# Three-layer kernel on one NeuronCore: layer norms by token tile, with the two matmul units ahead of them interleaved

## The reference

```
u = x @ w_in[l]                     # conv, two attentions, gates
m = g0 * conv(u) + g1 * diff_attention(u) + g2 * moba_attention(u)
x = layer_norm(ALPHA * x + m @ w_o[l])
h = square(relu(x @ w_ff1[l] + b_ff1[l]))
x = layer_norm(ALPHA * x + h @ w_ff2[l] + b_ff2[l])
```

## Time and profile before

| | |
|---|---|
| median of three runs | 1439.31 us |
| the profiled execution | 1438.97 us |
| its span, first to last instruction | 1437.2 us |
| TensorE busy | 1326.4 us (92%) |
| VectorE busy | 882.1 us (61%) |
| ScalarE busy | 599.6 us (42%) |
| mean granted TensorE clock | 0.963 |

### The profile page before, as it was taken

One profiled execution on the slowest core, in us unless ns is written; L12 is line 12 of the kernel. 1 busy time (PEld: TensorE's weight loads), 2 busy tenths in 40 slices (PEclk: granted clock), 3 DMA queues, 4 the chain that ended last, 5 costly groups with the idle time before them and its releaser, 6 DMA issues.

```text
span 1437.2 us, 22986 instructions
## 1 busy us (share of the span) xinstructions
PE 1326.4 (92%) x9406; PEld 1152.1 (80%) x9406; DVE 882.1 (61%) x1410; ACT 599.6 (42%) x957; POOL 33.1 (2%) x51
## 2 busy tenths in 40 slices
PE   7999989799999899998989999879889859999995
PEld 6999889698898799987979998778778746666563
DVE  3999867765555699985875545656874652222223
ACT  4346663444444434666435444435354322212211
POOL 1000000000000000000000000020040000000000
PEclk9999999999999999999999999979899969999998
DMA  9754435375555364443546555464346629999980
GB/s 291 251 177 145 142 88 160 132 231 189 175 185 194 124 226 150 148 134 100 172 147 199 197 179 199 143 193 147 105 145 225 226 117 377 415 419 419 415 355 31
DMA packets 172582, 289.96 MB, mean 202 GB/s; under 512 B 10324, under 2 KB 143076, under 8 KB 160204
## 3 DMA queue, kind: packets, MB, share of 16 engines
q1 hardware_dynamic: 169580, 281.55, 56.2%
q0 software_dynamic: 2752, 7.07, 1.7%
q10 hardware_dynamic: 160, 0.08, 0.0%
HBM read 287.61 MB, written 3.16 MB: 202 GB/s over the span
## 4 chain that ended last, share of the span: by engine, by line
PE 64%; DVE 26%; ACT 5%; issue 3%; DMA 1%; DVEq 0%; SPq 0%; ACTq 0%; POOL 0%
PE ps L1568 15%; PE ps L1569 14%; PE ps L1570 14%; DVE w_lo L995 8%; PE ps L1961 8%; DVE cvh L1113 5%; PE ps L1983 4%; ACT w_hi L630 3%; PE ps L1945 2%; PE ps L1992 2%; DVE nm L1071 1%; DVE x_nat L1044 1%; DVE gT L1036 1%; DVE ro L1105 1%; DVE ro L1101 1%
## 5 line engine op out<-in xcount | busy, mean ns | idle before, releaser
L995 DVE TENSOR_TENSOR w_lo<-raw,w_hi 128x2048 fp32r<-128x2048 f32 (+1 forms) x170 | 378.5, 2226 | 176.1 <-ACT w_hi L630 175.9
L630 ACT ACTIVATE w_hi<-raw 128x2048 fp32r<-128x2048 f32 (+1 forms) x170 | 316.8, 1864 | 265.7 <-PE ps L1570 259.4
L1568 PE MATMUL ps<-xT_hi,w_lo 128*128 128x256 f32 (+1 forms) x1224 | 356.7, 291 | 9.3 <-DVE xT_lo L1013 7.1
L1569 PE MATMUL ps<-xT_lo,w_hi 128*128 128x256 f32 (+1 forms) x1224 | 349.6, 286 | 0.0
L1570 PE MATMUL ps<-xT_hi,w_hi 128*128 128x256 f32 (+1 forms) x1224 | 349.2, 285 | 0.0
L1568 PEld LDWEIGHTS ps<-xT_hi,w_lo 128*128 128x128 f32 (+1 forms) x1224 | 237.1, 194 | 20.7 <-issue 11.7
L1569 PEld LDWEIGHTS ps<-xT_lo,w_hi 128*128 128x128 f32 (+1 forms) x1224 | 237.4, 194 | 0.5
L1570 PEld LDWEIGHTS ps<-xT_hi,w_hi 128*128 128x128 f32 (+1 forms) x1224 | 237.0, 194 | 0.2
L1568 PE MATMUL ps<-w_hi,xT_lo 128*128 128x256 f32 (+2 forms) x560 | 171.2, 306 | 2.0 <-DVE w_lo L995 1.7
L1569 PE MATMUL ps<-w_lo,xT_hi 128*128 128x256 f32 (+2 forms) x560 | 168.4, 301 | 0.0
L1570 PE MATMUL ps<-w_hi,xT_hi 128*128 128x256 f32 (+2 forms) x560 | 168.4, 301 | 0.0
(11 more groups left out here) (367 smaller groups left out, 1893.3 us busy)
## 6 DMA issues: line engine op xcount, KB each, us to landing
raw<-in_w_in SPq DMA_DIRECT2D x72, 1024.0 KB, 5.1
raw<-in_w_ff SPq DMA_DIRECT2D x64, 1024.0 KB, 5.2
raw<-in_w_gate SPq DMA_DIRECT2D x10, 1024.0 KB, 7.4
raw<-in_w_up SPq DMA_DIRECT2D x10, 1024.0 KB, 8.9
w_exp<-in_w_down SPq DMA_DIRECT2D x10, 1024.0 KB, 9.9
raw<-in_w_o SPq DMA_DIRECT2D x8, 1024.0 KB, 4.9
w_exp<-in_w_gate SPq DMA_DIRECT2D x8, 1024.0 KB, 9.1
raw<-in_w_down SPq DMA_DIRECT2D x8, 1024.0 KB, 10.3
```

What stands on the lines that cost most here:

```text
L630: nc.scalar.activation(w_hi[:, u % SPLIT, 0:n], raw[:, u % RAW, 0:n], ACT.Copy).then_inc(hi_done, 1)
L995: nc.vector.tensor_tensor(w_lo[:, u % SPLIT, 0:n], raw[:, u % RAW, 0:n], w_hi[:, u % SPLIT, 0:n].bitcast(F32), ALU.subtract).then_inc(spli ...
L1568: nc.tensor.matmul(out_, left[1], right[0], start=start, stop=False)
L1569: nc.tensor.matmul(out_, left[0], right[1], start=False, stop=False)
```

## The change

- **Last two units by tile** (`last_rows`). Of the two units ahead of a layer norm, TensorE now does: tile 0 of the first, tile 0 of the second, tile 1 of the first, tile 1 of the second. The second unit's operands are waited for after tile 0 of the first.
- **A third slot** (`w_ext`). The second of these units is split into a part of `br_hi` and `br_lo` that is free then, and the units after it change slots, so that the next stage's first unit can be split ahead of the norm.
- **The norm by tile.** Mean, squares, inverse root (`rsqrt_row`, 8 tiny steps for one tile) and outputs of tile 0 come ahead of the additions of tile 1.
- **Transposes by tile and half** (`turn`): one PSUM bank holds the four transposed blocks of one tile and half. In the third layer the order is half first.
- **High parts first.** The first column block of the first unit after a norm does its 16 matmuls with `xT_hi` first, and then the 8 with `xT_lo`. It waits for three of four parts of `xT_hi` (two in the third layer).
- The load of the third layer's first gain is released one output earlier.

```diff
+        BY_TILE = [(a, h) for a in range(TT) for h in range(2)]
+        BY_HALF = [(a, h) for h in range(2) for a in range(TT)]
+
+        def turned(a, h):
+
+            return ps[:, ACC + 2 * a + h, :].rearrange("p (c t) -> p c t", c=4)
+
+        def xT_part(x, a, h):
+
+            return x[:, 4 * h:4 * h + 4, a * P:(a + 1) * P]
+
+        w_ext = [x[:, 1:3].rearrange("p b c t -> p (b c t)") for x in (br_hi, br_lo)]
+
+        def split_of(u):
+
+            if u in (U_WO + 3, UNITS - 1):
+                return w_ext
+            slot = (u + (U_WO + 3 < u < UNITS - 1)) % SPLIT
+            return w_hi[:, slot, :], w_lo[:, slot, :]
+
+        def slot_user(u):
+
+            if u in (U_WO + 3, UNITS - 1):
+                return U_WO - 1
+            return u - 3 if u in (U_FF, U_FF + 1, UNITS, UNITS + 1) else u - 2
...
             def hi(base, u, n=UCOLS, i=None):
 
-                turn = (base + u) if i is None else (base + i + u)
-                act.wait_ge(unit_done, turn + 1)
-                nc.scalar.activation(w_hi[:, u % SPLIT, 0:n], raw[:, u % RAW, 0:n], ACT.Copy).then_inc(hi_done, 1)
+                turn = base + slot_user(u)
+                act.wait_ge(unit_done, (turn if i is None else turn + i) + 1 + SPLIT_CREDIT)
+                nc.scalar.activation(split_of(u)[0][:, 0:n], raw[:, u % RAW, 0:n], ACT.Copy).then_inc(hi_done, 1)
...
-                squares(0)
+                squares(0, 0)
                 split_hi(U_FF + 1)
+                squares(0, 1)
...
+                for q in range(2):
+                    u = UNITS - 5 + 2 * q
+                    relu(u, FFJ - 2 + q, 0, q)
+                    split_hi(u + 2)
+                    square_hi(FFJ - 2 + q, q)
+                    split_hi(u + 3)
+                squares(1, 0)
                 split_hi(UNITS + 1)
+                squares(1, 1)
...
+            def rsqrt_row(total, n, eps, v, y, z):
+
+                link(nc.vector.tensor_scalar(v, total, -(2.0 ** 26) / n, -(2.0 ** 26) * eps, ALU.mult, ALU.add))
+                link(nc.vector.tensor_scalar(y.bitcast(I32), v.bitcast(I32), -0.5, float(0x1F3759DF), ALU.mult, ALU.add))
+                for c in (3.0, 12.0, 768.0):
+                    link(nc.vector.scalar_tensor_tensor(out=z, in0=y, scalar=y, in1=v, op0=ALU.mult, op1=ALU.mult))
+                    link(nc.vector.scalar_tensor_tensor(out=y, in0=z, scalar=c, in1=y, op0=ALU.add, op1=ALU.mult))
...
-                    dve.wait_ge(ln_var, l * 2 * TT + k * TT + TT)
-                    link(last)
-                    link(nc.vector.tensor_scalar(nw[:, 0, 0:TT], ln_sq[:], 1.0 / D, LN_EPS, ALU.mult, ALU.add))
-                    rsqrt(nw[:, 0, 0:TT], nw[:, 1, 0:TT], nw[:, 2, 0:TT])
-                    for h in range(2):
-                        cols = slice(h * BANK, (h + 1) * BANK)
-                        for a in range(TT):
+                        dve.wait_ge(ln_var, l * 2 * TT + k * TT + a + 1)
+                        link(last)
+                        rsqrt_row(ln_sq[:, a:a + 1], D, LN_EPS, *[nw[:, i, a:a + 1] for i in range(3)])
+                        for h in range(2):
+                            cols = slice(h * BANK, (h + 1) * BANK)
                             nc.vector.scalar_tensor_tensor(out=x_nat[:, a, cols], in0=ln_y[:, a, cols], scalar=nw[:, 1, a:a + 1], in1=lnb[:, 1, cols], op0=ALU.mult, op1=ALU.add).then_inc(x_out, 1)
...
+                for k in range(3):
                     split(base, U_WO + k + 2, UCOLS)
                 layer_norm(0, U_WO + 3)
-                split(base, U_FF)
...
+                for q in range(2):
+                    u = UNITS - 5 + 2 * q
+                    square(FFJ - 2 + q, q)
+                    split(base, u + 2)
+                    square_lo(FFJ - 2 + q, q)
+                    split(base, u + 3)
                 layer_norm(1, UNITS - 1)
-                split(base, UNITS)
...
+                if ready is not None:
+                    o = ps[:, bank, 0:T]
+                    for k in range(KC):
+                        if k % 4 == 0:
+                            pe.wait_ge(xT_hid, ready[k // 4])
+                        nc.tensor.matmul(o, w[1][:, k, 0:P], xT[0][:, k, :], start=k == 0, stop=False)
+                        nc.tensor.matmul(o, w[0][:, k, 0:P], xT[0][:, k, :], start=False, stop=False)
+                    for k in range(KC):
+                        if k % 4 == 0:
+                            pe.wait_ge(xT_lod, ready[k // 4])
+                        nc.tensor.matmul(o, w[0][:, k, 0:P], xT[1][:, k, :], start=False, stop=k == KC - 1)
...
+            def last_rows(u, left, second_ready, second_left):
+
                 for a in range(TT):
                     for h in range(2):
-                        for k in range(2):
-                            last = mm3(ps[:, ACC + 2 * a + h, :], [x[:, k, a * P:(a + 1) * P] for x in left],
-                                       [x[:, k, h * BANK:(h + 1) * BANK] for x in w], start and k == 0, stop and k == 1)
-                        if stop and (a, h) != (TT - 1, 1):
-                            last.then_inc(tile_done, 1)
-                last.then_inc(unit_done, 1)
+                        last = rows_part(u, a, h, left, False, False)
+                    if a == 0:
+                        second_ready()
+                    else:
+                        last.then_inc(unit_done, 1)
+                    for h in range(2):
+                        last = rows_part(u + 1, a, h, second_left, False, True)
+                        last.then_inc(unit_done if (a, h) == (TT - 1, 1) else tile_done, 1)
...
+                def turn(a, h):
+                    for c in range(4):
+                        last = nc.tensor.transpose(turned(a, h)[:, c, :], x_nat[:, a, (4 * h + c) * P:(4 * h + c + 1) * P], ident[:])
+                    last.then_inc(xT_done, 1)
...
                 def make_xT(k):
-                    for half in range(2):
-                        pe.wait_ge(x_out, l * 8 + 4 * k + 2 * half + 1)
-                        for c in range(4 * half, 4 * half + 4):
-                            for a in range(TT):
-                                last = nc.tensor.transpose(ps[:, ACC + c // 2, (c % 2) * T + a * P:(c % 2) * T + (a + 1) * P], x_nat[:, a, c * P:(c + 1) * P], ident[:])
-                            if c % 2 == 1:
-                                last.then_inc(xT_done, 1)
+                    for b, (a, h) in enumerate(BY_TILE):
+                        pe.wait_ge(x_out, X_CREDIT + l * 8 + 4 * (k - 1) + b + 1)
+                        turn(a, h)
...
+                for a, h in BY_HALF:
+                    cols = slice(h * BANK, (h + 1) * BANK)
+                    nc.vector.scalar_tensor_tensor(out=dst[:, a, cols], in0=x_nat[:, a, cols], scalar=nw[:, 1, a:a + 1], in1=gain[:, cols], op0=ALU.mult, op1=ALU.mult).then_inc(normed, 1)
...
+                m_of = [[x[:, 2 * k:2 * k + 2, :] for x in xT] for k in range(4)]
+                for k in range(2):
+                    mixed_ready(k)
+                    rows_unit(U_WO + k, m_of[k], k == 0, False)
+                mixed_ready(2)
+                last_rows(U_WO + 2, m_of[2], lambda: mixed_ready(3), m_of[3])
                 make_xT(1)
...
+                for q in range(2):
+                    u = UNITS - 5 + 2 * q
+                    ready(u)
+                    pe.wait_ge(evac_a, l * EV_A + EV_A_IN + FFJ - 4 + q + 1)
+                    transposed(u, 4 + q, xT)
+                    if q == 0:
+                        ff2(1, u + 1, 0, FFJ - 3)
+                ff2_ready(UNITS - 2, 0, FFJ - 2)
+                last_rows(UNITS - 2, (h_hi[:, 0], h_lo[:, 0]), lambda: ff2_ready(UNITS - 1, 0, FFJ - 1), (h_hi[:, 1], h_lo[:, 1]))
```

More of the change, by code:

```diff
@@ L819, in make_xT2 @@
             def make_xT2(k):
-                for b in range(4):
+                for b, (a, h) in enumerate(BY_HALF):
                     act.wait_ge(xT_done, LAYERS * 8 + k * 4 + b + 1)
-                    nc.scalar.activation(xT_hi[:, 2 * b:2 * b + 2, :], ps[:, ACC + b, :].rearrange("p (c t) -> p c t", c=2), ACT.Copy).then_inc(xT_hid, 1)
-            square_sums(x_nat, 0, (-1, 0))
+                    nc.scalar.activation(xT_part(xT_hi, a, h), turned(a, h), ACT.Copy).then_inc(xT_hid, 1)
+            square_sums(x_nat, 0, (-2, 0))
             make_xT2(0)
@@ L1010, in make_xT @@
                 def make_xT(k):
-                    for b in range(4):
+                    for b, (a, h) in enumerate(BY_TILE):
                         dve.wait_ge(xT_hid, l * 8 + k * 4 + b + 1)
-                        nc.vector.tensor_tensor(xT_lo[:, 2 * b:2 * b + 2, :], ps[:, ACC + b, :].rearrange("p (c t) -> p c t", c=2),
-                                                xT_hi[:, 2 * b:2 * b + 2, :].bitcast(F32), ALU.subtract).then_inc(xT_lod, 1)
+                        nc.vector.tensor_tensor(xT_part(xT_lo, a, h), turned(a, h), xT_part(xT_hi, a, h).bitcast(F32), ALU.subtract).then_inc(xT_lod, 1)
```

(28 more changed lines are left out.)

65 lines of the change are left out of this document (35 added, 30 removed).

## The result

Five runs of the changed kernel gave 1431.04 to 1432.05 us, median **1431.47 us**; five of the kernel before beside them 1437.79 to 1442.16, median 1439.59. The ratio is 0.9943, 95% interval 0.9930 to 0.9956. The prediction, 1438.0 us in a range of 1432.8 to 1441.4, was too slow by 6.5 us, and the time lies under the range. The profiled execution took 1432.05 us with a span of 1430.3 (before 1438.97 and 1437.2), so 6.9 us have to be found in the two traces.

The account below looks back on a forecast made before the run. TensorE carries 64% of the chain and VectorE 26%, so shortening TensorE's idle time counts if the clock holds. Terms -3.8 + 2.9 + 1.0 - 0.6 - 0.4 = -0.9 us gave 1438.0 us, range 1432.8 to 1441.4.

Parts of the forecast that it names:

- The rest: Router (-0.6) and start (-0.4); otherwise same counts of matmuls, splits and loads, so nothing elsewhere.
- the prediction's own signs of being wrong: Stall shorter than 2 us, clock at 1.0 through it, or first matmul later than E+8.5.
- E: End of the last matmul ahead of a norm; in first norms the next matmul was forecast at E+7.2.
- First norms: First norm of each layer: gain 3.1 less 1.2 of clock loss, 1.9 us each; two give -3.8.
- Stalls: TensorE waits 3.3 us for the second w_ff2 unit's operand: +2.8 delay and +2.0 clock in each layer.
- Second norm, layer 0: Norm behind layer 0's feed-forward: gain 1.9; with delay 2.8 and clock 2.0, +2.9 us.
- Into the third layer: Layer 1's second norm into the RMS norm: gain 3.8; with delay 2.8 and clock 2.0, +1.0 us.
- Router: Ahead of the router, tile 0's product in halves lets transposes start 0.62 earlier: -0.6 us.
- Start: First matmul at the start no longer waits for xT_lo, 0.65 earlier, mostly at the low rate: -0.4 us.
- The first rival: Feed-forward stalls cost no clock (or only one does): 1434.1 us, 1431 with matmuls behind norms at full speed; chance 0.27.
- No stall: Second w_ff2 unit's operands come in time, both 2.8 and both 2.0 go: -10.5, 1428.5 us; chance 0.04.

Follow-up runs that it names:

- the one-chain kernel: Changed kernel with both tiles' inverse roots in one chain behind both products: 1440.55 us, ratio 0.9986; runs in two groups, 1434.97 to 1435.47 and 1440.16 to 1442.08.
- the kernel with the 16 matmuls: Changed kernel with 16 unread matmuls of 512 columns between the transposes of tile 0 and tile 1 in every layer norm: 1427.61 us.
- the kernel with the operand ahead: Changed kernel with rounding and splitting of the last w_ff2 unit's weights moved ahead of the last ReLU and square: 1426.62 us, ratio 0.9905.

## Why the prediction was wrong

**The step that failed** is "The rest. ... Same counts of matmuls, splits and loads otherwise: nothing." It carries 4.8 of the 6.0 us by which the sum (-0.9) missed the two traces (-6.9). None of the prediction's own signs of being wrong came: the stall was 3.01 us, the clock fell behind it, and the first matmul came at E+7.4.

- 2.2 of them are VectorE's wait behind the jumped-over block. This is shown: it goes with a shift of the code by 32 instructions, comes back with 256, and came back in the one-chain kernel. It is no merit of the change; another edit that moves VectorE's code can bring or cost it.
- 2.6 are low stretches of the clock in places that the change doesn't touch. TensorE's busy time at the low clock accounts for them. That the time of one program can change by as much is shown by the two groups of the one-chain kernel and by the changed one itself, whose slower runs have the lower mean clock. Why these three stretches came out well is open: both traces of the changed kernel have them alike and no other trace has all three, but both were taken of runs with its higher mean clock (0.967), and its median, 1.9 us higher at the second time, says that they need not be. With the changed kernel's second median the gain to before is 6.7 us instead of 8.1.

**Where the change lies**, the terms held: -2.1 against -0.9.
- First norms: -1.5 and -2.0 for -1.9. First matmul at E+7.4, low clock over 3.1 us of matmuls; the loss is 1.5 where I took 1.2.
- Stalls: 3.01 us for 3.3, because the operand came 5.92 us behind the last `w_ff1` unit instead of 6.05, and the 12 matmuls lasted 2.9 us. Delay and clock together 4.2 and 4.1 for 4.8. The clock's part was oversized: low for 3.4 us, which is 1.7 and not 2.0.
- Second norm, layer 0: -1.5 for -1.9. Into the third layer: -4.7 for -3.8, the largest miss among these terms. The transposes of `w_uk` come at 952.24, E+19.8 for E+20.4: the clock rose at 946.2, during the RMS transposes, and not behind them.
- Router: -0.8 for -0.6. Start: the first matmul was 0.56 us earlier, but the clock rose at 17.8 instead of 17.2, and nothing was left of the 0.4.
- The first rival (stalls that cost no clock) gives nearly the measured time, 1434.1 to 1431 (by its own terms, 3 x 1.2 further down from 1434.1, rather 1430.5), and is not what happened in the changed kernel's traces: the clock fell behind both stalls. In the kernel with the 16 matmuls and in the one with high parts first undone it did not fall, at the same 3.01 us. So neither my reading of the earlier trace rows, that every such stall costs, nor the strict one of the Trainium skill ("TensorE: Matmul & The Clock Gate", table of states), that none so short does, holds in general.
- "No stall" was given 1428.5; the kernel with the operand ahead came to 1426.6, and that gain was there to be had by moving one call in each of two queues.

My range was too narrow for the same reason: it took the single low stretches of the earlier trace rows as prices, and spent no width on the low stretches elsewhere. The three runs that I had differed by 1.8 us; the later ones of the kernel before differ by 8.

## What to carry to other kernels

Interleaving two units pays only where the second one's operand is ready: look first at how far behind the last producer it is, and move its preparation ahead in the queues; here that was worth 4.9 us, while the interleaving of the same units, without it, cost time. A step that shortens TensorE's idle time can be worth more than its length, or nothing, since it also moves the matmuls against the clock's rise (undoing the `w_o` interleaving cost 3.1 us a layer, and 0.65 us of wait went with 1.8); price it with a version that keeps TensorE busy, and in several runs, and read each run's mean clock beside its time. Before a few microseconds are put down to an edit, look for waits "<-issue" behind jumps that differ between the two kernels.
